# A hybrid decoder layer on one core: the activations f split once in w_up instead of tile by tile in w_down

## The reference

```python
x = x + jnp.einsum('bte,ed->btd', y_mix, w_out)
h2 = rmsnorm(x, norm_mlp_g)
f = jax.nn.relu(jnp.einsum('btd,df->btf', h2, w_up))      # 2048 -> 8192
x = x + jnp.einsum('btf,fd->btd', f * f, w_down)          # 8192 -> 2048
y = rmsnorm(x, norm_final_g)
```

## Time and profile before

| | |
|---|---|
| median of 3 runs | 1841.14 us (1840.48 to 1842.76) |
| the profiled execution | 1843.33 us, its span 1841.4 us |
| PE busy | 1812.1 us, 98% |
| DVE busy | 1478.1 us, 80% |
| ACT busy | 924.6 us, 50% |
| POOL busy | 132.9 us, 7% |
| DMA, the whole span | 288.19 MB, 157 GB/s |

### The profile page before, as it was taken

One profiled execution on the slowest core, in us unless ns is written; L12 is line 12 of the kernel. 1 busy time (PEld: TensorE's weight loads), 2 busy tenths in 40 slices (PEclk: granted clock), 3 DMA queues, 4 the chain that ended last, 5 costly groups with the idle time before them and its releaser, 6 DMA issues. The chain is left out here.

```text
span 1841.4 us, 38079 instructions
## 1 busy us (share of the span) xinstructions
PE 1812.1 (98%) x15016; PEld 1805.0 (98%) x15016; DVE 1478.1 (80%) x2039; ACT 924.6 (50%) x1322; POOL 132.9 (7%) x224
## 2 busy tenths in 40 slices
PE   7999999999999999999999999899999999999998
PEld 7999999999999999999999999899999999999998
DVE  7777785545488888888888888899888888889897
ACT  6555533333344454454445445555555555556565
POOL 3000000200000000000000000110000000001100
PEclk9999999999999999999999999999999999999999
DMA  8333333344354444544444452788666776767742
GB/s 275 103 92 91 97 98 93 116 152 139 99 171 148 160 146 163 173 135 156 148 161 146 143 173 90 213 233 238 185 179 179 199 181 181 192 168 206 230 114 93
DMA packets 209979, 288.19 MB, mean 157 GB/s; under 512 B 9437, under 2 KB 186089, under 8 KB 209808
## 3 DMA queue, kind: packets, MB, share of 16 engines
q1 hardware_dynamic: 185552, 186.75, 33.0%
q0 software_dynamic: 23984, 99.19, 18.7%
q10 hardware_dynamic: 288, 0.11, 0.0%
HBM read 222.00 MB, written 64.53 MB: 156 GB/s over the span
## 5 line engine op out<-in xcount | busy, mean ns | idle before, releaser
L897 PE MATMUL ps<-forms,u_high 128*128 128x260 f32 x2688 | 490.4, 282 | 0.7 <-DVE product_parts L1833 0.7
L897 PEld LDWEIGHTS ps<-forms,u_high 128*128 128x128 f32 x2688 | 413.0, 188 | 0.9 <-issue 0.9
L897 PE MATMUL ps<-forms,u_low 128*128 128x260 f32 x1344 | 374.8, 282 | 0.6 <-DVE u_low L1823 0.6
L897 PE MATMUL ps<-forms,d_high 128*128 128x260 f32 x2240 | 373.6, 283 | 1.0 <-DVE product_parts L1833 1.0
L897 PEld LDWEIGHTS ps<-forms,d_high 128*128 128x128 f32 x2240 | 314.4, 188 | 1.2 <-ACT d_high L1180 1.1
L897 PE MATMUL ps<-f_forms,d_high 128*128 128x260 f32 x1344 | 265.4, 283 | 4.2 <-ACT d_high L1180 1.6
L897 PEld LDWEIGHTS ps<-forms,u_low 128*128 128x128 f32 x1344 | 250.7, 188 | 0.8 <-DVE u_low L1823 0.8
L1363 DVE TENSOR_TENSOR w_low<-raw,w_high 128x512 fp32r<-128x512 f32 x160 | 109.0, 689 | 137.0 <-ACT w_high L992 135.8
L897 PEld LDWEIGHTS ps<-f_forms,d_high 128*128 128x128 f32 x1344 | 204.9, 188 | 6.7 <-ACT d_high L1180 3.7
L897 PE MATMUL ps<-forms,d_low 128*128 128x260 f32 x1120 | 192.5, 283 | 0.0
L992 ACT ACTIVATE w_high<-raw 128x512 fp32r<-128x512 f32 x160 | 99.4, 628 | 180.7 <-PE ps L704 174.6
(11 more groups left out here) (305 smaller groups left out, 3578.5 us busy)
## 6 DMA issues: line engine op xcount, KB each, us to landing
even_rows<-in_w_up_dram SPq DMA_DIRECT2D x32, 1024.0 KB, 5.6
odd_rows<-in_w_up_dram SPq DMA_DIRECT2D x32, 1024.0 KB, 5.8
d_even<-in_w_down_dram SPq DMA_DIRECT2D x33, 768.0 KB, 7.1
d_odd<-in_w_down_dram SPq DMA_DIRECT2D x33, 768.0 KB, 5.2
raw<-in_w_in_dram SPq DMA_DIRECT2D x96, 256.0 KB, 2.7
sums_spill<-part_out POOLq DMA_DIRECT2D x40, 520.0 KB, 5.4
scratch<-f_spill POOLq DMA_DIRECT2D x20, 910.0 KB, 7.1
f_spill<-f_out POOLq DMA_DIRECT2D x32, 520.0 KB, 4.7
```

The costliest lines, as they stand in the source:

```text
L897: mm = pe.matmul(out, w[:, k, :], x[:, form, :], start=(PRODUCT_OPENS[r] and at == 0), stop=at == len(steps) - 1, skip_group_check=True)
```

## The change

The four blocks and three sums of f are split in w_up, right after they are made: ACT writes the high part of all seven forms into one buffer (`split_high`, in turn 6 of the next pair), DVE overwrites the forms with their low parts (`split_low`, in turn 0 of the pair after that). `f_scale` and `f_sums` go from turns 5 and 6 to turns 4 and 5. `send_f` sends high and low parts; memory now holds both (`parts_dram`). In w_down, `load_forms` reads a tile's high and low parts straight into its set, in two pieces (forms 0 to 2, forms 3 to 6), which PE waits for itself; `window_high` and `window_low` are gone. Tile 1 comes in four pieces, since it lies where forms of the last pair are still in use.

Loads are paced: tiles 4 and later wait until a given segment's products are done (`SENT_FOR`). The last pair but one (30) is sent, and the fourth tile (3) loaded, after the first segment's sums. Pair 30 keeps its sums in the places of the odd pairs, so that the weights of segment 0 may come earlier; they and those of segment 1 change places. The last pair (31) is finished in segments 6 to 8. The cut of the fourth segment is 3 tiles instead of 4. DVE waits once, in segment 4, for pair 30 to be sent. At the very end, six tiles of the output instead of four go ahead of the second norm.

```diff
-        (0, 3, 9, 15, 21, 26, 32), (0, 4, 10, 16, 22, 26, 32), (0, 4, 10, 16, 22, 26, 32), (0, 5, 11, 17, 23, 27, 32))
+        (0, 3, 9, 15, 21, 26, 32), (0, 3, 9, 15, 21, 26, 32), (0, 4, 10, 16, 22, 26, 32), (0, 5, 11, 17, 23, 27, 32))
...
+SENT_FOR = {_kp: LAST_USE[_kp - D_SETS] if _kp >= D_SETS else FIRST_USE[_kp] - (3 if _kp < D_SETS - 1 else 2)
+            for _kp in range(4, DOWN_KP)}
-SQUARES_AT, SCALE_AT, SUMS_SEG = first_q(3) + 3, first_q(3) + 6, 6
+SQUARES_AT, SCALE_AT, SUMS_SEG = first_q(6) + 3, first_q(7) + 6, 8
...
-OUT_BANKS, LATE_TOTALS = (1, 2, 3, 4, 6, 7, 5), 3
+OUT_BANKS, LATE_TOTALS = (1, 2, 3, 4, 6, 7, 5), 5
...
-                    if seg < 2:
+                    if seg == 0:
+                        sp.wait_ge(f_out_sent[0], SENT[UP_PAIRS - 4])
+                    elif seg == 1:
                         sp.wait_ge(u_lo, UP_Q)
-                        if seg == 1:
-                            sp.wait_ge(f_out_sent[i], SENT[UP_PAIRS - 2 - i])
...
+            def load_piece(kp, piece):
+                first, end = (PIECES_1 if kp == 1 else PIECES)[piece]
+                pool.dma_start(f_forms[kp % D_SETS][:, :, first:end, :].bitcast(F32),
+                               parts_dram[kp, :, :, first:end, :]).then_inc(forms_in[kp % D_SETS][piece], 16)
+
+            def load_forms(kp):
+                pool.wait_ge(split_sent, 16 * (kp + 1))
+                pool.wait_ge(f_out_sent[kp % 2], SENT[kp])
                 if kp == 0:
...
+                    pool.wait_ge(u_lo, UP_Q - PRODUCTS)
+                elif kp == 1:
+                    pool.wait_ge(u_used, UP_Q - 3)
                 else:
...
+                    pool.wait_ge(u_used, UP_Q)
+                if kp >= 4:
+                    pool.wait_ge(u_used, first_q(SENT_FOR[kp] + 1))
+                load_piece(kp, 0)
+                load_piece(kp, 1)
+                if kp == 1:
+                    pool.wait_ge(u_used, UP_Q - 1)
+                    load_piece(kp, 2)
+                    pool.wait_ge(u_used, UP_Q)
+                    load_piece(kp, 3)
...
             def send_f(m):
                 pool.wait_ge(f_ready, m + 1)
...
+                to = parts_dram[m, :, 1]
+                pool.dma_start(parts_dram[m, :, 0], f_high).then_inc(split_sent, 16)
+                pool.dma_start(to[:, 0:4, :], f_out[m % 2][:]).then_inc(f_out_sent[m % 2], 16)
...
+            for m in range(UP_PAIRS - 2):
                 send_f(m)
...
+            for kp in range(3):
+                load_forms(kp)
...
+            for seg in range(FIRST_FINAL):
+                if seg == 1:
+                    send_f(UP_PAIRS - 2)
+                    load_forms(3)
                 if seg == SUMS_SEG:
                     send_f(UP_PAIRS - 1)
...
+                for kp in range(4, DOWN_KP):
+                    if SENT_FOR[kp] == seg:
+                        load_forms(kp)
+                send_sums(seg)
...
-                        if r < 2 and FIRST_USE[kp] == m - UP_PAIRS:
-                            pe.wait_ge(f_hi, 2 * kp + r + 1)
+                        if FIRST_USE[kp] == m - UP_PAIRS and r in ((0, 1, 4, 6) if kp == 1 else (0, 1)):
+                            pe.wait_ge(forms_in[kp % D_SETS][(0, 1, 4, 6).index(r)], 16 * (kp // D_SETS + 1))
...
-                    act.wait_ge(sums_sent[seg % 2], 16 * (seg // 2))
+                    act.wait_ge(x2_out[seg % 2], sums_sent(seg // 2))
...
+            def split_high(m):
+
+                act.wait_ge(f_summed, m + 1)
+                act.wait_ge(split_sent, 16 * m)
+                for part, first, end in split_parts(m):
+                    act.activation(f_high[:, first:end, :].bitcast(F32R), part, ACT.Copy).then_inc(split_hi, 1)
...
+                if r == 6 and 1 <= m < UP_PAIRS:
+                    split_high(m - 1)
+                if turn == first_q(SUMS_SEG) + 1:
+                    split_high(UP_PAIRS - 1)
...
+                    if m == UP_PAIRS + 4:
+                        dve.wait_ge(f_out_sent[0], SENT[UP_PAIRS - 2])
...
+            def split_low(m):
+
+                dve.wait_ge(f_summed, m + 1)
+                for n, (part, first, end) in enumerate(split_parts(m)):
+                    dve.wait_ge(split_hi, split_count(m) + n + 1)
+                    if end == FORMS:
+                        settle()
+                    ins = dve.tensor_tensor(part.bitcast(F32R), part, f_high[:, first:end, :], ALU.subtract)
...
+                if r == 0 and 2 <= m <= UP_PAIRS:
+                    split_low(m - 2)
+                if turn == first_q(SUMS_SEG) + 2:
+                    split_low(UP_PAIRS - 1)
...
+                if 1 <= m < UP_PAIRS and r == 4:
+                    f_scale(m - 1)
                 if 1 <= m < UP_PAIRS and r == 5:
-                    f_scale(m - 1)
-                if 1 <= m < UP_PAIRS and r == 6:
                     f_sums(m - 1)
...
-            y_tile(1)
-            y_tile(3)
+            for m in (1, 3, 5):
+                y_tile(m)
             half_norm(1)
```

More of the change, by code:

```diff
@@ L103, in which_product, with in_odd_place @@
     return (LAST_ORDER if q >= first_q(LAST) else IN_ORDER)[q % PRODUCTS]
[L107 to L123, removed]
-SQUARES_AT, SCALE_AT, SUMS_SEG = first_q(3) + 3, first_q(3) + 6, 6
+for _kp in range(D_SETS, DOWN_KP):
+    assert LAST_USE[_kp - D_SETS] + 1 < FIRST_USE[_kp]
+SENT_FOR = {_kp: LAST_USE[_kp - D_SETS] if _kp >= D_SETS else FIRST_USE[_kp] - (3 if _kp < D_SETS - 1 else 2)
+            for _kp in range(4, DOWN_KP)}
+SQUARES_AT, SCALE_AT, SUMS_SEG = first_q(6) + 3, first_q(7) + 6, 8
+def in_odd_place(m):
+    return m < UP_PAIRS - 1 and (m % 2 == 1 or m == UP_PAIRS - 2)
 SENT = {}
 for _m in range(UP_PAIRS):
-    SENT[_m] = SENT.get(_m - 2, 0) + 16 * (3 if _m % 2 and _m < UP_PAIRS - 1 else 2)
+    SENT[_m] = SENT.get(_m - 2, 0) + 16 * (3 if in_odd_place(_m) else 2)
 GROUP_ORDER = sorted(range(4), key=lambda c: max(FINALS.index(2 * c), FINALS.index(2 * c + 1)))
@@ L365, in build, with sums_sent @@
         x2_out = [sem(f"x2_out{b}") for b in range(2)]
+        def sums_sent(count):
+            return 16 * (OUT_PAIRS // 2 + count)
         pair_evac = sem("pair_evac")
@@ L401, in form_rows, with split_parts, split_count @@
                 return tuple(end_sums[:, n, :] for n in range(3))
-            if m % 2 == 0:
+            if not in_odd_place(m):
                 return tuple(even_sums[:, n, :] for n in range(3))
             return odd_sums[:, 0, :], odd_sums[:, 1, :], odd_sum[:]
+        def split_parts(m):
+            if m == UP_PAIRS - 1:
+                return (f_out[1][:], 0, 4), (end_sums[:], 4, 7)
+            if not in_odd_place(m):
+                return (f_out[0][:], 0, 4), (even_sums[:], 4, 7)
+            return (f_out[m % 2][:], 0, 4), (odd_sums[:], 4, 6), (odd_sum[:].unsqueeze(1), 6, 7)
+        def split_count(m):
+            return sum(3 if in_odd_place(k) else 2 for k in range(m))
         def blocks_at(q):
@@ L891, in product @@
                         pe.wait_ge(s_lo, 2 * k + 2)
-                    if kind == 1 and k == 0 and r < 2 and m >= UP_PAIRS and FIRST_USE[end - 1] == m - UP_PAIRS:
-                        pe.wait_ge(f_lo, 2 * (end - 1) + r + 1)
                     if kind == 2 and k == 0:
@@ L1309, in _ @@
                 seg = m - UP_PAIRS
-                if turn == UP_Q:
-                    window_high(1, 0)
-                    window_high(1, 1)
                 weights_high(turn)
                 up_copies(turn)
-                for part in range(2):
-                    if turn - part in FORMS_AT:
-                        window_high(FORMS_AT[turn - part], part)
+                if r == 6 and 1 <= m < UP_PAIRS:
+                    split_high(m - 1)
+                if turn == first_q(SUMS_SEG) + 1:
+                    split_high(UP_PAIRS - 1)
                 if turn == first_q(LAST) + 2:
@@ L1972, in _ @@
                     f_sums(UP_PAIRS - 1)
-                for part in range(2):
-                    if turn - 2 - part in FORMS_AT:
-                        window_low(FORMS_AT[turn - 2 - part], part)
                 if seg > FIRST_FINAL and r == 3:
@@ L2039, in _ @@
                               ALU.add).then_inc(samples_sq, 1)
-            y_tile(1)
-            y_tile(3)
+            for m in (1, 3, 5):
+                y_tile(m)
             half_norm(1)
-            for m in range(5, 16, 2):
+            for m in range(7, 16, 2):
                 y_tile(m)
```

106 lines of the change are left out of this document (32 added, 74 removed).

## The result

The changed kernel takes **1846.52 us** (median of 14 runs, 1844.44 to 1848.69), the kernel before 1842.41 (14 runs, 1840.48 to 1847.6): a ratio of 1.0023, 95% interval 1.0016 to 1.0031. It is 4.1 us slower, where 4.4 us faster had been forecast.

What follows compares the result with a forecast made beforehand. PE bounds the kernel, so only its standing time can be won: 11.7 us lost in w_down's first eight segments becomes 7.3, 4.4 won, 1841.14 - 4.4 = 1836.7 us (chance 0.45, own range 1834 to 1840); overall range 1832 to 1845.

Steps and rivals of the forecast that it cites:

- Splitting in w_up (cost 0): In w_up, DVE gets 2.1 us more per pair, 19.2 of 20.1, and ACT 1.8; cost on the path 0.
- Segments 0 and 1 without splitting (1.0 and 0.8 lost): Start of w_down: segment 0 loses its 1.0 us again, segment 1 about 0.8 instead of 3.5.
- the last rival: Segment 0: tile 1's pieces land too late and PE waits, 1 to 2 us, 1838; chance inside the forecast's 0.45.
- the landing at T0 + 2.5: Segment 0: tile 1's last piece lands some 2.5 us after T0 (start of w_down), wanted at 4.3.
- the terms of the sum: Ramp of w_down: 0.37 MB/us for loads, sends and weights; first data about 1.4 us after T0 (start of w_down).
- The order of service (by age): Ramp of w_down: the two DMA queues are served by age of issue, not in turns; 7.3 us lost instead of 11.7.
- The first rival (turns, 1841.8): Ramp of w_down: queues take turns, weights slip ahead of sums 1; 12.4 us lost, 0.7 more than before; chance 0.22.
- the third rival: Ramp of w_down: DMA slower than its best stretches; 20 us lost, 1849, or halfway 1845; chance 0.13.
- The ledger: Ramp transfers by age, after T0 (start of w_down): tile 2 to 9.3 us, sums 1 landed 27.9, sums 2 38.8.
- the forecast's crux, product 6 of segment 3: Segment 3 of w_down: this product waits for sums 1, starting 28.9 us after w_down's start against 24.0 undisturbed.
- The rest (0): Later w_down and the end: later tiles cost 0 to 1 us, taken as 0; the end also 0.
- The end: End of kernel: one more output tile stored before the second norm, between 0.5 us won and 0.3 lost, taken as 0.

Runs made afterwards that it cites:

- the run without the wait for tile 1: Changed kernel, with PE reading tile 0's forms in place of tile 1's in segments 0 and 1 and waiting for tile 1 only in segment 2: 1844.53 us, 1.0011.
- the first run with one queue: Changed kernel, with POOL instead of SP issuing the weights of segments 2 to 7, in one queue with f and the sums: 1839.75 us, 0.9987.
- the three runs with five pieces: Changed kernel, tile 1 in five pieces, pair 30 sent earlier: two queues 1842.98 us; one queue for f, sums, weights 1836.39; that with pair 30 in halves 1834.59.
- the run with small packets: Changed kernel, f's parts stored with gaps to shrink packets, each piece loaded as two transfers; f's packets stayed 3.6 KB: 1854.70 us, 1.0066.

## Why the prediction was wrong, point by point

**Splitting in w_up (cost 0): right.** No PE time is lost there. DVE was forecast at 19.2 of 20.1 us, 0.955, and measured at 0.956 of 500 us. Over 25 pairs DVE's split took 57.1 us, 2.3 a pair for 2.1 forecast (and 0.1 more for odd pairs), ACT's 50.4, 2.0 for 1.8. In all DVE was busy for 52.5 us more than before in that row, 2.1 a pair. (By its own rows, the prediction's 842.8 for the next u_low should be 842.5, which changes nothing.) The largest pieces:

```profile
L1930 DVE TENSOR_TENSOR f_out<-f_out,scratch 128x1040 fp32r<-128x1040 f32 x25 | 30.8, 1233 | 0.0
L1322 ACT ACTIVATE scratch<-f_out 128x1040 fp32r<-128x1040 f32 x25 | 26.9, 1076 | 0.3
```

**Segments 0 and 1 without splitting (1.0 and 0.8 lost): right about DVE, as the run without the wait for tile 1 shows (0.6 and 0.8)**, but the piece of tile 1 that the last rival priced at 1 to 2 us cost 3.7 and the clock behind it 2.0 in segment 0. The step that failed there is the landing at T0 + 2.5. The last two pieces landed at T0 + 6.9 and 8.7: POOL issued the first of them, 0.53 MB that the sum had as moved before T0, only at T0 + 0.1, though the product that it waits for was over at T0 - 2.7; on an otherwise idle DMA (the first run with one queue) both needed 4.2 us from issue to landing, where the terms of the sum give 3.2 for 0.53 MB and 2.5 for 0.27; and with two queues the weights of segment 2 took turns with them.

**The order of service (by age): the step that failed, and with it the sign.** I read it from a stretch in which the weights had 0.92 of the engines and the sums 0.14 and said that both queues had work. They had not: from 1185.6 to 1186.9 the weights' queue moved 487 packets and the other one 1:

```profile
q1 hardware_dynamic: 487, 0.48, 106.6%
q0 software_dynamic: 1, 0.00, 1.6%
```

So the sums issued at 1182.77 had not yet reached the engines: their first packet moved at 1186.9, and the 32 packets are the end of the sums before and the beginning of these. A stretch 1 us later, in the same trace of before, shows the turns (the queues from 1187.9 to 1190.1):

```profile
q0 software_dynamic: 94, 0.37, 85.0%
q1 hardware_dynamic: 111, 0.11, 18.2%
```

About as many packets, and 0.37 against 0.11 MB. The rule that I had weighed and set aside (the Trainium skill, "DMA: Bandwidth & Descriptors", section "Queues, rings and completion order": each engine serves its queues in turn, one packet at a time) agrees with these rows and with the 803 against 784 packets of after. I had looked at shares, where the packets had to be counted.

**The first rival (turns, 1841.8) had the rule and not the victim.** It priced the sums as late, because weights slip in ahead of them. With packets four times as small it is the weights that starve. PE stood waiting for them 2.5 us ahead of segment 3, 4.9 inside it, and 1.2 in segment 4, and the sums' wait hardly showed. That the sharing between two queues is the cause, and not the number of bytes (the third rival), is shown by two runs: half the bytes in the loads changed little (1845.7), one queue for the same bytes won 6.6 us (the ratios 1.0023 and 0.9987). "Sharing" here takes in both the turns and the late first packet; and in POOL's queue the weights' packets are also four times as large (last section). These the runs do not separate.

**The ledger itself** can be judged where the weights of segments 2 to 7 stand in its queue. There the first data moved at T0 + 1.5, for 1.4 forecast. But the last piece of tile 1 landed at T0 + 5.0, not 2.5, and tile 2 at T0 + 14.3, for 9.3 and 0.4 to its landing. The start was the mis-sized term: 0.53 MB more stood ahead, and up to T0 + 6.6 the DMA moved 214 GB/s (0.21 MB/us) at 0.69 of its engines, waits for the first data included:

```profile
1163.23:1169.83 6.60, 5.54 (x45) 5.15 (x43) 4.93 (x14) 3.75 (x10) 4.32 (x6) 1.00 0.69 214
```

Behind it the rates were a little better than forecast: 2.5 us for sums instead of 3.0, 11.7 for the 4.51 MB instead of 12.2. So the ledger was 4.6 us late at tile 2, 3.0 at sums 1 (T0 + 30.9, not 27.9) and 2.0 at sums 2. Product 6 of segment 3 began at T0 + 32.9 for 28.9 forecast; the other 1.0 is DVE, whose low part and sum follow ACT's copy (the copy was over at 1194.6, the sum at 1196.0). Sums 2 landed at T0 + 40.8 (38.8 forecast), when PE was by then too late to wait for them. So the forecast's crux, product 6 of segment 3, appears as soon as there is one queue; 10.3 us are lost instead of 7.3.

**The rest (0).** Later tiles cost nothing, right: from segment 9 to the end 4.1 us are lost, 4.6 before. The end was put between 0.5 won and 0.3 lost; about 1 was won.

The range ended at 1845, 1.5 short; 1.3 of this is the base, since before has a median of 1842.41 over 14 runs where the three runs shown had 1841.14. The range left out most of the cases in which the DMA does worse than now, though the ramp's DMA was named as full.

## What to carry to other kernels

Where two queues share the DMA, count packets, not bytes or shares: a queue of 1 KB packets beside one of 4 KB packets gets a fifth of the bytes, and what is small and urgent starves behind what is large and early. Before a load is doubled in a stretch whose DMA is full, ask which transfer of *another* queue will then be late; where order matters, put both into one queue and write the order out. A loss that is taken away in front of a late transfer comes back as a longer wait for it, so judge such an edit by the start of the first segment behind the crowded stretch, not by the wait that it removes.

## What the hardware showed that I had not expected

**The software queue joins rows.** The weights' rows of 1 KB travel in packets of 1.0 KB from SP's queue (784 packets, 0.78 MB) but in some 4 KB from POOL's: the first run with one queue had 997 packets for 4.00 MB of f, sums and weights from 1182 to 1194, and by their sizes in the trace those of the weights hold 4096 bytes, four rows each. So moving weights there also frees them from small packets; which share of the gain is order and which is packet size was not tried. The Trainium skill ("DMA: Bandwidth & Descriptors", section "SWDGE vs HWDGE vs iDMA") says that a packet is preferably at most 4096 bytes, and that its end is the point where an engine changes from one context to another. The equal numbers of packets agree with the second. On the size, the packets of POOL's queue were 4096 bytes for the weights and mostly 4160 to 7280 for f and sums, at that size or above it, and those of SP's queue, at 1.0 KB, far below.

**A pause of POOL.** In the changed kernel and the six runs that keep its list up to there, POOL stood 6.44 us between the second and third transfer of tile 1 and then issued 2.8 us after the product that it waits for was over, with nothing in the profile to wait for. Where the first two pieces were four transfers, the next was issued 0.3 us after that product's end. In the three runs with five pieces, POOL again issued the third transfer 2.8 us after the product that it waited for. The row of the changed kernel, and of the run with small packets (start, us, instruction, idle before):

```profile
1162.72 1.42 POOL L643 DMA_DIRECT2D forms<-f_parts_spill  x2 [6.44 <-issue]
```

```profile
1160.43 1.44 POOL L644 DMA_DIRECT2D forms<-f_parts_spill  x2 [2.87 <-PE ps L924]
```

What POOL does in that time stays open.
